# The scan of a two-block transformer kernel on one Trainium2 core: two carried parts added on VectorE before they reach TensorE

## The chip, the cores and the metric

The kernel runs on one core of one Trainium2 chip, in one launch. The metric is the device time of that launch in microseconds (us). Work is shared among five engines that have queues of their own and meet only at semaphores: TensorE (PE in the profile; its weight loads are PEld), VectorE (DVE), ScalarE (ACT), GpSimd (POOL) and SyncE (SP), which issues the DMAs. SBUF is the on-chip memory; PSUM, with eight banks of 512 f32 words per partition, takes the results of TensorE. Each queue is worked off in order, so an instruction that waits holds up all behind it on its engine.

## What is computed

Two transformer layers come first, with feed-forward parts, three kinds of attention and gates. A second block follows, on 256 tokens, and only one stage of it is touched: the bidirectional scan. For one direction, cut to what matters (chunks of 128 tokens, so two chunks; 12 heads of 64 channels in 4 groups that share B and C of 128 states):

```python
st = einsum('bcsgn,bcsgr,bcsgrp->bcgrpn', Bq, exp(a_end - a_cs), xq)      # what a chunk adds to the state
h_fin, h_in = scan(step, h0, (st, a_end))                                # state carried into each chunk
scores = einsum('bcqgn,bcsgn->bcqsg', Cq, Bq)                            # C and B
y_diag = einsum('bcqsg,bcqsgr,bcsgrp->bcqgrp', scores, decay, xq)        # within the chunk
y_off  = einsum('bcqgn,bcgrpn,bcqgr->bcqgrp', Cq, h_in, exp(a_cs))       # carried into the chunk
y = y_diag + y_off
```

This is done forward and backward and the two y are added. Then y + d_skip * x is gated by silu(z), normed over 768 channels and multiplied by the output weights, and the block goes on with a feed-forward part.

## The kernel before, in words

Activations lie with channels on the partitions and 256 tokens along the free dimension. Weights stream through a ring of five slabs of 128x2048 (`raw`); ScalarE writes the high part of each to `whi`, VectorE or GpSimd the rest to `wlo` (`cut_lo`; on GpSimd as two halves), and each f32 product is three matmuls (`block3`).

The scan has four steps e = 0 to 3: token chunk tt = e // 2, direction d = e % 2. For each step:

- `carried(e)` (TensorE, L1717): C times the carried state of the direction, 4 matmuls into PSUM banks 6 and 7.
- `carried_scale(e)` (VectorE, L2504): that product times exp(a_cs) per token and head, out of PSUM into `yoff` in SBUF, tokens on the partitions.
- `turned(e)` (TensorE, L1726): `yoff` times the identity, 6 matmuls, which turns it to channels on the partitions and adds it to y in banks 0 to 2. `turned(0)` opens the banks (start=True).
- `within_weights(e)` (VectorE, L2495): the decays `seg[e]` (128x1536) times the scores in PSUM, in place.
- `within(e)` (TensorE, L1735): 12 matmuls of 64 channels each that add the part within the chunk. Those of step 3 release `y_done`, three times.

The scores of both chunks (L1709, 8 matmuls, `cb_done`) come ahead of all this. The order on each engine is written out by hand. `carried(e)` waits until step e-1 has been read out of banks 6 and 7 (`yoff_ready`).

Between the steps VectorE has other work: `z_clamp(j)` for j = 1, 2 (L2455, 128x512), a clamp of z into `zex`, of which ScalarE makes a sigmoid (`z_sigmoid`, three activations) and GpSimd the product with z (`silu` of z, L633, `z_silu`). All three j share the one tile `zex`, so `z_clamp(1)` waits for `z_silu` 1, the product of j = 0, and `z_clamp(2)` for `z_silu` 2. GpSimd's queue here is: the fourfold product `xdt` (L544), the z product 0, the z product 1, the two halves of slab WOUT20+2, the z product 2, the two halves of slab WOUT20+3. VectorE also has `cut_lo` of slab WOUT20+1 (128x2048) and `ycat_low(0, ...)`, the low part of `u_t` (128x512, `hlo`).

Behind step 3 VectorE adds the skip part (L2531), multiplies by the gate, ScalarE squares, TensorE sums (L1574) while it works on the parts of the output product that are there (`wout`, L1165 to L1167), and the norm follows.

Of the kernel before, what the change touches and what calls it, by code (L numbers as in the profile page):

```python
# [18 lines left out]
ALU = mybir.AluOpType  # L19
# [3 lines left out]
P = 128  # L23
D = 1024
KT = D // P
S = 256
ST = S // P
# [24 lines left out]
WOUT20 = WIN20 + WIN2_SLABS  # L52
# [80 lines left out]
class Steps:  # L133
# [32 lines left out]
NG = 4  # L166
# [9 lines left out]
def build_program(nc, t):  # L176
# [31 lines left out]
    ident = sb("ident", [P, P])  # L208
# [86 lines left out]
    yoff = at("yoff", [P, 2, 768], F32, xw0)  # L295
# [20 lines left out]
    b_t = at("b_t", [P, NG, S], F32, a0 + 12288)  # L316
# [9 lines left out]
    xdt = at("xdt", [P, ST, 2, 768], F32, v0)  # L326
# [816 lines left out]
    def _(pe):  # L1143
# [559 lines left out]

        pe.wait_ge(conv_silu, NCONV)
        pe.wait_ge(h1_ready, 1)
        for tt in range(ST):
            for g in range(NG):
                tok = slice(tt * P, (tt + 1) * P)
                ins = pe.matmul(ps[:, 4 + tt, g * P:(g + 1) * P], b_t[:, g, tok], c_t[:, g, tok], start=True, stop=True)  # L1709
        ins.then_inc(cb_done, 1)  # L1710

        def carried(e):

            tt, d = e // 2, e % 2
            at_least(pe, yoff_ready, e)
            for g in range(NG):
                ins = pe.matmul(ps[:, 6 + g // 2, 192 * (g % 2):192 * (g % 2) + 192], c_t[:, g, tt * P:(tt + 1) * P],  # L1717
                                hstate[:, d, (tt if d == 0 else 1 - tt), 192 * g:192 * g + 192], start=True, stop=True)
            ins.then_inc(yoff_done, 1)

        def turned(e):

            tt = e // 2
            pe.wait_ge(yoff_ready, e + 1)
            for m in range(XC):
                pe.matmul(ps_flat[:, m * S + tt * P:m * S + (tt + 1) * P], yoff[:, e % 2, m * P:(m + 1) * P], ident[:, :],  # L1726
                          start=(e == 0 and m % 2 == 0), stop=False, skip_group_check=True)

        def within(e):

            tt, d = e // 2, e % 2
            pe.wait_ge(seg_ready, e + 1)
            for h in range(NH):
                out = ps[64 * (h % 2):64 * (h % 2) + 64, h // 4, (h // 2 % 2) * S + tt * P:(h // 2 % 2) * S + (tt + 1) * P]
                ins = pe.matmul(out, xdt[:, tt, d, 64 * h:64 * h + 64], seg[e][:, h, :], start=False, stop=(d == 1),  # L1735
                                skip_group_check=True)
                if e == 3 and h % 4 == 3:
                    ins.then_inc(y_done, 1)

        carried(0)  # L1740
        pe.wait_ge(uz_evac, 8)
        turned(0)
        carried(1)
        pe.wait_ge(xdt_ready, 1)
        within(0)
        turned(1)
        carried(2)
        within(1)
        turned(2)
        carried(3)  # L1750
        within(2)
        turned(3)
        within(3)

        def wout(q, first, last):
# [71 lines left out]
    def _(dve):  # L1827
# [3 lines left out]
        def tt_(out, a, b, op):  # L1831
            return dve.tensor_tensor(out, a, b, op)  # L1832
# [7 lines left out]
        def cut_lo(g):  # L1840

            if N_SLABS <= g < CTX0:
                return
            slot = PLACE[g] % NS
            dve.wait_ge(hi_done[slot], SPLITS[g])
            c = slice(PART if g in DT_SLABS else 0, SLAB)
            tt_(wlo[:, slot, c], raw[:, slot, c], whi[:, slot, c].bitcast(F32), ALU.subtract).then_inc(lo_done[slot], 1)
# [647 lines left out]
        def within_weights(e):  # L2495

            tt = e // 2
            s4 = seg[e][:, :, :].rearrange("p (g r) n -> p g r n", r=3)
            dve.wait_ge(cb_done, 1)
            dve.wait_ge(seg_exp, 3 * tt + 3)  # L2500
            tt_(s4, s4, ps[:, 4 + tt, :].rearrange("p (g n) -> p g n", n=P).unsqueeze(2).to_broadcast([P, NG, 3, P]),
                ALU.mult).then_inc(seg_ready, 1)

        def carried_scale(e):  # L2504

            dve.wait_ge(yoff_done, e + 1)
            form = "p b (h n) -> p b h n"
            tt_(yoff[:, e % 2, :].rearrange("p (b h n) -> p b h n", b=2, n=64), ps[:, 6:8, 0:384].rearrange(form, n=64),
                tail_x[:, 48 + 12 * e:60 + 12 * e].rearrange("p (b h) -> p b h", b=2).unsqueeze(3).to_broadcast([P, 2, 6, 64]),
                ALU.mult).then_inc(yoff_ready, 1)  # L2510

        def ycat_low(j, first, src):
            dve.wait_ge(ycat_hi_ready, j + 1)
# [3 lines left out]
        for e in range(4):  # L2517
            if e == 3:
                ycat_low(0, 0, u_t[:, :, :])
            carried_scale(e)  # L2520
            within_weights(e)
            if e == 0:
                z_clamp(1)
                cut_lo(b2 + WOUT20 + 1)
            if e == 1:
                z_clamp(2)

        for j in range(XC // 2):
            dve.wait_ge(y_done, j + 1)
# [240 lines left out]
```

## Time and profile before

| | us |
|---|---|
| runs of the kernel before | median 1632.33 (1631.1 to 1632.45) |
| the profiled execution | 1631.88 |
| its span in the trace | 1630.1 |
| TensorE matmuls busy | 1610.9 (99%) |
| VectorE busy | 1295.7 (79%) |
| ScalarE busy | 923.4 (57%) |
| GpSimd busy | 205.5 (13%) |
| stage of the scan (scores to the last within product) | 1380.15 to 1401.11 |

The times of rows are microseconds from the start of the span. A row of the timeline has the start, the length, the engine, the line, the operation, the tiles and the count; in brackets stands how long the engine was idle before it, and who ended that. Each f32 matmul shows as two passes, so x12 is six matmuls. An instruction of VectorE or GpSimd can begin some hundredths before the last one ends, and its length holds the time in which it is already issued but can't move.

### The profile page before, as it was taken

What the parts mean: (1) busy time and instruction counts of PE and PEld (TensorE: products, weight loads), DVE (VectorE), ACT (ScalarE), POOL (GpSimd) and SP (SyncE); (2) the same over time, 40 slices, a digit from 0 to 9 for tenths busy, and PEclk for the clock granted to TensorE, in tenths of its full rate; (3) what the DMA queues carried; (4) which work ended last, traced back from release to release, by engine and by line L of the source; (5) the groups of instructions that cost most, each with busy time, mean ns of one, the idle gap of its engine ahead of it and who ended that gap; (6) DMA issues with size and microseconds to landing.
All of it is one profiled execution on the core that took longest, in us unless ns stands there. A gap on an engine that the chain in (4) does not pass through costs nothing.

```text
span 1630.1 us, 29907 instructions
## 1 busy us (share of the span) xinstructions
PE 1610.9 (99%) x13152; PEld 1546.7 (95%) x13152; DVE 1295.7 (79%) x1458; ACT 923.4 (57%) x1094; POOL 205.5 (13%) x122
## 2 busy tenths in 40 slices
PE   8999999999999999999999999999999999999998
PEld 8999978999999999999988899999999988999998
DVE  8887878678889888897878678875898598796655
ACT  7554655675465455545656685464555557554544
POOL 1000100000140001200100000032323358400000
PEclk9999999999999999999999999999999999999999
DMA  7667654344556765776654434555554424135552
GB/s 293 230 259 288 236 185 175 140 146 159 219 220 235 279 237 198 283 259 253 264 187 175 150 134 158 193 217 191 197 198 165 152 107 155 70 138 185 204 185 75
DMA packets 47521, 317.58 MB, mean 195 GB/s; under 512 B 5280, under 2 KB 8096, under 8 KB 9888
## 3 DMA queue, kind: packets, MB, share of 16 engines
q1 hardware_dynamic: 47248, 315.64, 52.8%
q8 instruction: 104, 1.70, 0.4%
q14 instruction: 25, 0.20, 0.0%
q10 hardware_dynamic: 144, 0.02, 0.0%
HBM read 314.60 MB, written 1.05 MB: 194 GB/s over the span
## 4 chain that ended last, share of the span: by engine, by line
PE 90%; DVE 7%; ACT 2%; issue 1%; DMA 1%; SPq 0%; DVEq 0%; ACTq 0%
PE ps L1165 25%; PE ps L1166 25%; PE ps L1167 25%; PE ps L1363 3%; PE ps L1365 3%; PE ps L1364 3%; DVE wlo L1832 2%; PE ps L1377 1%; DVE pre L2443 1%; PE ps L1388 1%; DVE dA_rows L1832 1%; DVE tmp L1832 1%; DMA raw<-in_w_dram 1%; DVE qkA L1832 1%; PE ps L1584 0%
## 5 line engine op out<-in xcount | busy, mean ns | idle before, releaser
L1832 DVE TENSOR_TENSOR wlo<-raw,whi 128x2048 fp32r<-128x2048 f32 (+1 forms) x256 | 584.8, 2292 | 90.4 <-ACT whi L649 87.3
L649 ACT ACTIVATE whi<-raw 128x2048 fp32r<-128x2048 f32 (+1 forms) x264 | 500.1, 1906 | 215.0 <-DMA raw<-in_w_dram 214.6
L1165 PE MATMUL ps<-h1hi,whi 128*128 128x256 f32 x1792 | 500.2, 279 | 3.4 <-DVE wlo L1832 3.4
L1167 PE MATMUL ps<-h1lo,whi 128*128 128x256 f32 x1792 | 496.2, 277 | 0.0
L1166 PE MATMUL ps<-h1hi,wlo 128*128 128x256 f32 x1792 | 496.2, 277 | 0.0
L1165 PEld LDWEIGHTS ps<-h1hi,whi 128*128 128x128 f32 x1792 | 336.8, 188 | 7.0 <-DVE h1lo L1891 2.5
L1166 PEld LDWEIGHTS ps<-h1hi,wlo 128*128 128x128 f32 x1792 | 336.8, 188 | 0.1
L1167 PEld LDWEIGHTS ps<-h1lo,whi 128*128 128x128 f32 x1792 | 336.9, 188 | 0.0
L1165 PE MATMUL ps<-hid_hi,whi 128*128 128x256 f32 x880 | 243.7, 277 | 0.0
L1166 PE MATMUL ps<-hid_hi,wlo 128*128 128x256 f32 x880 | 243.0, 276 | 0.0
L1167 PE MATMUL ps<-hid_lo,whi 128*128 128x256 f32 x880 | 243.0, 276 | 0.0
L1165 PE MATMUL ps<-hhi,whi 128*128 128x256 f32 x672 | 188.1, 280 | 2.3 <-DVE hlo L2418 1.3
L1166 PE MATMUL ps<-hhi,wlo 128*128 128x256 f32 x672 | 186.2, 277 | 0.0
L1167 PE MATMUL ps<-hlo,whi 128*128 128x256 f32 x672 | 186.2, 277 | 0.0
L1165 PEld LDWEIGHTS ps<-hid_hi,whi 128*128 128x128 f32 x880 | 165.2, 188 | 0.3
L1166 PEld LDWEIGHTS ps<-hid_hi,wlo 128*128 128x128 f32 x880 | 165.3, 188 | 0.0
L1167 PEld LDWEIGHTS ps<-hid_lo,whi 128*128 128x128 f32 x880 | 165.2, 188 | 0.0
L550 POOL TENSOR_TENSOR sq<-sq 128x512 f32<-128x512 f32 x18 | 27.5, 1528 | 934.4 <-ACT sq L678 922.6
L1165 PEld LDWEIGHTS ps<-hhi,whi 128*128 128x128 f32 x672 | 126.6, 188 | 4.1 <-issue 2.3
L1166 PEld LDWEIGHTS ps<-hhi,wlo 128*128 128x128 f32 x672 | 126.3, 188 | 0.3
L1167 PEld LDWEIGHTS ps<-hlo,whi 128*128 128x128 f32 x672 | 126.2, 188 | 0.0
L683 ACT ACTIVATE t_exp<-t_exp 128x512 f32<-128x512 f32 x55 | 34.7, 632 | 145.2 <-DVE t_exp L1986 145.1
(365 smaller groups left out, 2624.8 us busy)
## 6 DMA issues: line engine op xcount, KB each, us to landing
raw<-in_w_dram SPq DMA_DIRECT2D x288, 1024.0 KB, 4.8
raw<-in_w_dram SPq DMA_DIRECT2D x8, 256.0 KB, 5.2
c_rows<-in_c_rows_dram SPq DMA_DIRECT2D x2, 1024.0 KB, 9.9
relbias<-in_relbias_dram SPq DMA_DIRECT2D x2, 1024.0 KB, 8.5
pv<-in_pv_dram SPq DMA_DIRECT2D x2, 641.0 KB, 6.9
xT<-in_x_dram SPq DMA_DIRECT2D x4, 256.0 KB, 4.6
raw<-in_w_dram SPq DMA_DIRECT2D x2, 512.0 KB, 6.0
ctxT<-in_ctx_dram SPq DMA_DIRECT2D x1, 1024.0 KB, 6.8
```

Of the source, the lines that this page charges most:

```text
L550: step.done(pool.tensor_tensor(sq[:, 0:2, :], sq[:, 0:2, :], sq[:, 2 * j:2 * j + 2, :], ALU.add))
L649: act.activation(whi[:, slot, c], raw[:, slot, c], ACT.Copy).then_inc(hi_done[slot], 1)
L683: step.done(act.activation(v, v, ACT.Exp, scale=-1.0))
L1165: pe.matmul(out, w_hi, hi, start=start, stop=False, skip_group_check=skip)
L1166: pe.matmul(out, w_lo, hi, start=False, stop=False, skip_group_check=skip)
L1167: return pe.matmul(out, w_hi, lo, start=False, stop=stop, skip_group_check=skip)
L1363: pe.matmul(out, h_hi, w_hi, start=(k == 0), stop=False)
L1364: pe.matmul(out, h_hi, w_lo, start=False, stop=False)
L1365: ins = pe.matmul(out, h_lo, w_hi, start=False, stop=(k == KT - 1))
L1377: ins = pe.transpose(ps_flat[:, first + j * P:first + (j + 1) * P], tile, ident[:, :])
L1388: ins = pe.matmul(ps_flat[:, c:c + width], qkT[rows, j, tt * P:(tt + 1) * P], qkT[rows, 4 + j, 0:width], start=True, stop=True)
L1832: return dve.tensor_tensor(out, a, b, op)
```

## The change

Three things are done.

1. The two directions of one chunk are added on VectorE. `carried_scale` for an even step writes the scaled product to `yoff[tt]` as before. For an odd step it scales the product in place in PSUM, waits for itself (`done`), and adds it to `yoff[tt]` in a further instruction. `turned` is then called twice, once for each chunk, in place of four times.
2. On TensorE `carried(0)` is put ahead of the scores, `carried(1)` behind them, `within(0)` opens the banks of y (start=True on the first matmul of each bank and partition half), and `turned(tt)` comes behind `within(0)` and `within(2)`.
3. On VectorE `z_clamp(1)` is put ahead of `within_weights(0)` and the cut of slab WOUT20+1 behind `within_weights(2)`, in place of behind `z_clamp(1)`.

```diff
-        for tt in range(ST):
-            for g in range(NG):
-                ...
-        ins.then_inc(cb_done, 1)
...
-        def turned(e):
-            tt = e // 2
-            pe.wait_ge(yoff_ready, e + 1)
+        def turned(tt):
+            pe.wait_ge(yoff_ready, 2 * tt + 2)
             for m in range(XC):
-                pe.matmul(ps_flat[...], yoff[:, e % 2, m * P:(m + 1) * P], ident[:, :],
-                          start=(e == 0 and m % 2 == 0), stop=False, skip_group_check=True)
+                pe.matmul(ps_flat[...], yoff[:, tt, m * P:(m + 1) * P], ident[:, :],
+                          start=False, stop=False, skip_group_check=True)
...
-                ins = pe.matmul(out, xdt[...], seg[e][:, h, :], start=False, stop=(d == 1), ...)
+                ins = pe.matmul(out, xdt[...], seg[e][:, h, :], start=(e == 0 and h % 4 < 2), stop=(d == 1), ...)
...
         carried(0)
+        for tt in range(ST):
+            for g in range(NG):
+                tok = slice(tt * P, (tt + 1) * P)
+                ins = pe.matmul(ps[:, 4 + tt, ...], b_t[:, g, tok], c_t[:, g, tok], start=True, stop=True)
+        ins.then_inc(cb_done, 1)
+        carried(1)
         pe.wait_ge(uz_evac, 8)
-        turned(0)
-        carried(1)
         pe.wait_ge(xdt_ready, 1)
         within(0)
-        turned(1)
         carried(2)
+        turned(0)
         within(1)
-        turned(2)
         carried(3)
         within(2)
-        turned(3)
+        turned(1)
         within(3)
...
             dve.wait_ge(yoff_done, e + 1)
-            tt_(yoff[:, e % 2, :]..., ps[:, 6:8, 0:384]..., tail_x[...]..., ALU.mult).then_inc(yoff_ready, 1)
+            product = ps[:, 6:8, 0:384]
+            both = yoff[:, e // 2, :].rearrange("p (b m) -> p b m", b=2)
+            ins = tt_((product if e % 2 else both)..., product..., tail_x[...]..., ALU.mult)
+            if e % 2:
+                done(ins)
+                ins = tt_(both, both, product, ALU.add)
+            ins.then_inc(yoff_ready, 1)
...
             carried_scale(e)
-            within_weights(e)
             if e == 0:
                 z_clamp(1)
-                cut_lo(b2 + WOUT20 + 1)
+            within_weights(e)
             if e == 1:
                 z_clamp(2)
+            if e == 2:
+                cut_lo(b2 + WOUT20 + 1)
```

On TensorE, from the first scores on, stood this before (`c_t` and `b_t` are C and B, `hstate` the carried states, `seg0` to `seg3` the weights of steps 0 to 3):

```order
L1709 MATMUL ps<-c_t_151,b_t_139 128x128 x8
L1717 MATMUL ps<-hstate_140,c_t_151 128x192 x4
L1726 MATMUL ps<-ident_56,yoff_123 128x128 x6
L1717 MATMUL ps<-hstate_140,c_t_151 128x192 x4
L1735 MATMUL ps<-seg0_162,xdt_146 64x128 x12
L1726 MATMUL ps<-ident_56,yoff_123 128x128 x6
L1717 MATMUL ps<-hstate_140,c_t_151 128x192 x4
L1735 MATMUL ps<-seg1_163,xdt_146 64x128 x12
L1726 MATMUL ps<-ident_56,yoff_123 128x128 x6
L1717 MATMUL ps<-hstate_140,c_t_151 128x192 x4
L1735 MATMUL ps<-seg2_164,xdt_146 64x128 x12
L1726 MATMUL ps<-ident_56,yoff_123 128x128 x6
```

(one more group, of `seg3`, ends the stage), and this stands there now, the whole stage:

```order
L1712 MATMUL ps<-hstate_140,c_t_151 128x192 x4
L1738 MATMUL ps<-c_t_151,b_t_139 128x128 x8
L1712 MATMUL ps<-hstate_140,c_t_151 128x192 x4
L1729 MATMUL ps<-seg0_162,xdt_146 64x128 x12
L1712 MATMUL ps<-hstate_140,c_t_151 128x192 x4
L1720 MATMUL ps<-ident_56,yoff_123 128x128 x6
L1729 MATMUL ps<-seg1_163,xdt_146 64x128 x12
L1712 MATMUL ps<-hstate_140,c_t_151 128x192 x4
L1729 MATMUL ps<-seg2_164,xdt_146 64x128 x12
L1720 MATMUL ps<-ident_56,yoff_123 128x128 x6
L1729 MATMUL ps<-seg3_165,xdt_146 64x128 x12
```

Two of four groups of turning matmuls are gone, and a carried product stands on both sides of the scores.

On VectorE, behind the scaling of step 0, stood this before:

```order
L1832 TENSOR_TENSOR seg0_162<-seg0_162,ps 128x1536
L2455 TENSOR_SCALAR zex_136<-z_t_130 128x512
L1832 TENSOR_TENSOR wlo_50<-raw_49,whi_51 128x2048
L1832 TENSOR_TENSOR yoff_123<-ps,small2_160 128x768
L1832 TENSOR_TENSOR seg1_163<-seg1_163,ps 128x1536
L2455 TENSOR_SCALAR zex_136<-z_t_130 128x512
L1832 TENSOR_TENSOR yoff_123<-ps,small2_160 128x768
L1832 TENSOR_TENSOR seg2_164<-seg2_164,ps 128x1536
L1832 TENSOR_TENSOR hlo_55<-u_t_166,hhi_54 128x512
L1832 TENSOR_TENSOR yoff_123<-ps,small2_160 128x768
L1832 TENSOR_TENSOR seg3_165<-seg3_165,ps 128x1536
```

and now, up to the last addition (`seg3` is right behind it):

```order
L2452 TENSOR_SCALAR zex_136<-z_t_130 128x512
L1829 TENSOR_TENSOR seg0_162<-seg0_162,ps 128x1536
L1829 TENSOR_TENSOR ps<-ps,small2_160 128x2x384
L1829 TENSOR_TENSOR yoff_123<-yoff_123,ps 128x768
L1829 TENSOR_TENSOR seg1_163<-seg1_163,ps 128x1536
L2452 TENSOR_SCALAR zex_136<-z_t_130 128x512
L1829 TENSOR_TENSOR yoff_123<-ps,small2_160 128x768
L1829 TENSOR_TENSOR seg2_164<-seg2_164,ps 128x1536
L1829 TENSOR_TENSOR wlo_50<-raw_49,whi_51 128x2048
L1829 TENSOR_TENSOR hlo_55<-u_t_166,hhi_54 128x512
L1829 TENSOR_TENSOR ps<-ps,small2_160 128x2x384
L1829 TENSOR_TENSOR yoff_123<-yoff_123,ps 128x768
```

The clamp stands ahead of `seg0`, the cut of the slab has moved from ahead of step 1 to directly ahead of `hlo` and step 3, and each odd step has one instruction more. The queues of ScalarE, GpSimd and SyncE are as before.

## Rows read from the trace of the kernel before

**Rows 1.** The page, the chain that ended last, shares by engine.

```profile
PE 90%; DVE 7%; ACT 2%; issue 1%; DMA 1%; SPq 0%; DVEq 0%; ACTq 0%
```

**Rows 2.** Timeline of TensorE, the scan: start us, length us, engine, what.

```profile
1380.15 1.95 PE L1709 MATMUL ps<-c_t,b_t 128*128 128x128 f32 x16
1381.93 1.47 PE L1717 MATMUL ps<-hstate,c_t 128*128 128x192 f32 x8
1384.54 1.57 PE L1726 MATMUL ps<-ident,yoff 128*128 128x128 f32 x12 [1.14 <-DVE yoff L1832]
...
1387.35 1.53 PE L1735 MATMUL ps<-seg,xdt 128*64 128x128 f32 x24
1389.52 1.60 PE L1726 MATMUL ps<-ident,yoff 128*128 128x128 f32 x12 [0.64 <-DVE yoff L1832]
...
1399.65 1.53 PE L1735 MATMUL ps<-seg,xdt 128*64 128x128 f32 x24
1401.11 0.38 PE L1165 MATMUL ps<-hhi,whi 128*128 128x256 f32 x1
```

**Rows 3.** The chain of waits, a piece behind the scan: start us, us, what.

```profile
1404.20 2.63 PE ps L1574 x12
```

**Rows 4.** Timeline of VectorE, the scan and what follows it.

```profile
1383.44 0.96 DVE L1832 TENSOR_TENSOR yoff<-ps,small 128x768 f32<-128x768 f32 x1 [3.00 <-PE ps L1717]
1384.31 1.74 DVE L1832 TENSOR_TENSOR seg<-seg,ps 128x1536 f32<-128x1536 f32 x1
1385.97 0.42 DVE L2455 TENSOR_SCALAR zex<-z_t 128x512 f32<-128x512 f32 x1
1386.31 2.29 DVE L1832 TENSOR_TENSOR wlo<-raw,whi 128x2048 fp32r<-128x2048 f32 x1
...
1391.04 1.29 DVE L2455 TENSOR_SCALAR zex<-z_t 128x512 f32<-128x512 f32 x1
1392.46 0.96 DVE L1832 TENSOR_TENSOR yoff<-ps,small 128x768 f32<-128x768 f32 x1
...
1395.00 1.35 DVE L1832 TENSOR_TENSOR hlo<-u_t,hhi 128x512 fp32r<-128x512 f32 x1
...
1400.35 0.87 DVE L2531 SCALAR_TENSOR_TENSOR xs_t<-xs_t,pc,ps 128x256 f32<-128x256 f32 x2 [0.98 <-PE ps L1735]
...
1407.82 0.42 DVE L1836 SCALAR_TENSOR_TENSOR rsqb<-rsqa 128x256 f32<-128x256 f32 x1
1408.27 0.43 DVE L1832 TENSOR_TENSOR rsqb<-rsqb,var 128x256 f32<-128x256 f32 x1
```

**Rows 5.** Timeline of GpSimd, the scan.

```profile
1384.59 1.27 POOL L633 TENSOR_TENSOR z_t<-z_t,zex 128x512 f32<-128x512 f32 x1
...
1389.69 2.36 POOL L538 TENSOR_TENSOR wlo<-raw,whi 128x1024 fp32r<-128x1024 f32 x1
1392.00 2.56 POOL L538 TENSOR_TENSOR wlo<-raw,whi 128x1024 fp32r<-128x1024 f32 x1
1394.53 1.26 POOL L633 TENSOR_TENSOR z_t<-z_t,zex 128x512 f32<-128x512 f32 x1
1395.76 2.81 POOL L538 TENSOR_TENSOR wlo<-raw,whi 128x1024 fp32r<-128x1024 f32 x1
```

**Rows 6.** Timeline of VectorE, a feed-forward part some 190 us earlier.

```profile
1197.37 3.77 DVE L1832 TENSOR_TENSOR wlo<-raw,whi 128x2048 fp32r<-128x2048 f32 x1
1201.07 2.88 DVE L1832 TENSOR_TENSOR hid_lo<-t_hid,hid_hi 128x512 fp32r<-128x512 f32 x1
```

**Rows 7.** Timeline of GpSimd, the same stretch.

```profile
1196.14 2.85 POOL L538 TENSOR_TENSOR wlo<-raw,whi 128x1024 fp32r<-128x1024 f32 x1
1198.96 4.45 POOL L538 TENSOR_TENSOR wlo<-raw,whi 128x1024 fp32r<-128x1024 f32 x1
```

**Rows 8.** Busy by stretch (PE, PEld, DVE, ACT, POOL), then granted clock, DMA share, GB/s.

```profile
1380.00:1402.00 22.00, 20.22 (x202) 18.41 (x201) 17.45 (x17) 6.61 (x10) 18.28 (x10) 1.00 0.20 81
```

**Rows 9.** The waits of TensorE in the whole span: total, times, longest us.

```profile
PE ps L1270 <- issue: 1.8, 1, 1.8
```

More of the change, by code:

```diff
@@ L1705, in _ @@
         pe.wait_ge(h1_ready, 1)
-        for tt in range(ST):
-            for g in range(NG):
-                tok = slice(tt * P, (tt + 1) * P)
-                ins = pe.matmul(ps[:, 4 + tt, g * P:(g + 1) * P], b_t[:, g, tok], c_t[:, g, tok], start=True, stop=True)
-        ins.then_inc(cb_done, 1)
         def carried(e):
@@ L1719, in carried @@
             ins.then_inc(yoff_done, 1)
-        def turned(e):
-            tt = e // 2
-            pe.wait_ge(yoff_ready, e + 1)
+        def turned(tt):
+            pe.wait_ge(yoff_ready, 2 * tt + 2)
             for m in range(XC):
-                pe.matmul(ps_flat[:, m * S + tt * P:m * S + (tt + 1) * P], yoff[:, e % 2, m * P:(m + 1) * P], ident[:, :],
-                          start=(e == 0 and m % 2 == 0), stop=False, skip_group_check=True)
+                pe.matmul(ps_flat[:, m * S + tt * P:m * S + (tt + 1) * P], yoff[:, tt, m * P:(m + 1) * P], ident[:, :],
+                          start=False, stop=False, skip_group_check=True)
         def within(e):
@@ L1734, in within @@
                 out = ps[64 * (h % 2):64 * (h % 2) + 64, h // 4, (h // 2 % 2) * S + tt * P:(h // 2 % 2) * S + (tt + 1) * P]
-                ins = pe.matmul(out, xdt[:, tt, d, 64 * h:64 * h + 64], seg[e][:, h, :], start=False, stop=(d == 1),
-                                skip_group_check=True)
+                ins = pe.matmul(out, xdt[:, tt, d, 64 * h:64 * h + 64], seg[e][:, h, :], start=(e == 0 and h % 4 < 2),
+                                stop=(d == 1), skip_group_check=True)
                 if e == 3 and h % 4 == 3:
@@ L1740, in _ @@
         carried(0)
+        for tt in range(ST):
+            for g in range(NG):
+                tok = slice(tt * P, (tt + 1) * P)
+                ins = pe.matmul(ps[:, 4 + tt, g * P:(g + 1) * P], b_t[:, g, tok], c_t[:, g, tok], start=True, stop=True)
+        ins.then_inc(cb_done, 1)
+        carried(1)
         pe.wait_ge(uz_evac, 8)
-        turned(0)
-        carried(1)
         pe.wait_ge(xdt_ready, 1)
         within(0)
-        turned(1)
         carried(2)
+        turned(0)
         within(1)
-        turned(2)
         carried(3)
         within(2)
-        turned(3)
+        turned(1)
         within(3)
@@ L2507, in carried_scale @@
             form = "p b (h n) -> p b h n"
-            tt_(yoff[:, e % 2, :].rearrange("p (b h n) -> p b h n", b=2, n=64), ps[:, 6:8, 0:384].rearrange(form, n=64),
-                tail_x[:, 48 + 12 * e:60 + 12 * e].rearrange("p (b h) -> p b h", b=2).unsqueeze(3).to_broadcast([P, 2, 6, 64]),
-                ALU.mult).then_inc(yoff_ready, 1)
+            product = ps[:, 6:8, 0:384]
+            both = yoff[:, e // 2, :].rearrange("p (b m) -> p b m", b=2)
+            ins = tt_((product if e % 2 else both).rearrange(form, n=64), product.rearrange(form, n=64),
+                      tail_x[:, 48 + 12 * e:60 + 12 * e].rearrange("p (b h) -> p b h", b=2).unsqueeze(3)
+                      .to_broadcast([P, 2, 6, 64]), ALU.mult)
+            if e % 2:
+                done(ins)
+                ins = tt_(both, both, product, ALU.add)
+            ins.then_inc(yoff_ready, 1)
         def ycat_low(j, first, src):
```

## The prediction

> **What bounds the kernel now.** I read the page first. The chain that ended last is TensorE's for 90% of the span [rows 1], so a microsecond taken from TensorE counts only where TensorE is what the stage waits for, and one that it must wait anew counts in full. Then I laid the timelines of the stage side by side. TensorE goes from the scores at 1380.15 to the first output product at 1401.11, 20.96 us, and is idle twice, 1.14 and 0.64 us, each time for VectorE's `yoff` [rows 2]. So before, TensorE bounds the scan and VectorE is just behind: its clamp of z at 1391.04 is followed only at 1392.46 by the next scaling, as soon as the carried product is there. Behind the scan the chain goes on through the skip part at 1400.35 [rows 4] and the sums of squares [rows 3], so a delay of step 3 reaches the end of the kernel undiminished.
>
> **TensorE alone would gain.** Twelve turning matmuls go, two groups of 12 passes at about 1.41 us from start to start (I read 1.57 and 1.60 with the drain [rows 2]): 2.8 us. The two idle times, 1.8 us, could go too. That is the ceiling, 4.6 us. All of it is hidden if VectorE is late, so I walk VectorE's new queue.
>
> **VectorE, step by step.** An instruction starts some 0.08 us before the last ends, so I use start-to-start lengths: scaling 0.87, `seg` 1.66, clamp 0.34 (the first three rows and the fourth [rows 4]).
>
> 1. `carried(0)` now starts at 1380.15 and takes 1.47, so its scaling runs from 1381.66 instead of 1383.44 [rows 2, 4]. A head start of 1.8 us.
> 2. `z_clamp(1)` is next, and it waits for z product 0, since both use `zex`. GpSimd runs that from 1384.59 to 1385.86 [rows 5], and nothing in the change makes it earlier: it follows the `xdt` product in GpSimd's own queue. Before, the clamp stood at 1385.97, behind `seg0`, where the wait was already over [rows 4]. Now VectorE stands idle from 1382.6 to 1385.93, and `seg0` is queued behind the wait: it starts at 1386.27, not 1384.31, and `within(0)` at 1388.07, not 1387.35 [rows 2, 4]. The head start is gone and 0.7 us more. The scores end near 1383.5, so they hold up nothing.
> 3. Step 1: the scaling in PSUM from 1387.93, 0.96 long, then the addition. A dependent pair follows with a gap of 0.03 (1407.82 + 0.42 to 1408.27 [rows 4]). The addition also reads 768 elements, one operand from PSUM; I take 0.96 again. It ends at 1389.87. Neither instruction is in the trace. The bounds for each are 0.9 and 1.74, the latter a `seg` row, with twice the elements; I take 0.96, the row of the same size and the same source. Then `seg1` from 1389.8 to 1391.53.
> 4. `z_clamp(2)` is issued at 1391.45. Before, it was issued at 1391.04 and ended at 1392.33, 0.28 behind the end of GpSimd's half slab (1389.69 + 2.36 = 1392.05), though by itself it takes 0.42 [rows 4, 5]. The half slab of GpSimd holds it, and it does so again: end 1392.3. The scaling of step 2 starts at 1392.22 (its product, behind the addition of step 1, is ready at 1391.5), 0.24 earlier than before. `seg2` runs from 1393.1 to 1394.84.
> 5. The slab cut is issued at 1394.76. Before, it ran at 1386.31, where GpSimd was idle, in 2.29 us [rows 4]. Now GpSimd is in z product 2, until 1395.79 [rows 5], and its half slabs are queued behind that. What comes of this I read from an earlier place with the same three instructions [rows 6, 7]: a cut issued at 1197.37 waited for the GpSimd half that ended at 1198.99 and ended 2.15 later at 1201.14; the second half, issued at 1198.96, waited for it and took 4.45; and the 128x512 low part that VectorE issued at 1201.07 waited for that half and took 2.88, not 0.69 or so. So the two take turns, whole instructions long. Here: the cut ends at 1395.76 + 2.15 = 1397.9; `hlo`, issued at 1397.83, takes 2.88 and ends at 1400.71 (before: 1.35 at 1395.00 [rows 4]).
> 6. Step 3: scaling from 1400.63 to 1401.59, addition to 1402.58, `seg3` from 1402.5 to 1404.24, `within(3)` at 1404.3 against 1399.65 [rows 2].
>
> One rule speaks against this change. The trace has the turns: 3.77, 4.45 and 2.88 us [rows 6, 7]. The Trainium skill, "SBUF — State Buffer", section "SBUF: two separate sides", says that a VectorE instruction with two SBUF inputs or in a two-port mode and a GpSimd instruction share a pair of ports that one of them holds to its end. The trace agrees, and the forecast would be the same by it; what it adds is that the two new additions, with one input in PSUM, should pay nothing to GpSimd (if they did, each could wait up to a half slab, 2.4 us).
>
> **The sum.** Counted on VectorE's queue against the rows of before [rows 2, 4]:
> - up to the end of step 2: the head start of 1.8, the wait behind it, the cut out of this stretch and one addition into it leave VectorE 0.24 us earlier (1394.76 against 1395.00), since both times GpSimd's half slab releases the clamp;
> - the cut, now here: 1397.83 - 1394.76 = 3.07;
> - from `hlo`'s start to `within(3)`: before 1399.65 - 1395.00 = 4.65; now 2.80 for `hlo`, 0.99 for the scaling with its gap, 0.88 for the addition, 1.80 for `seg3` and its signal, 6.47 in all: 1.82 more.
>
> -0.24 + 3.07 + 1.82 = 4.65 us. TensorE's path fits below: it is done with `within(2)` at 1397.1 and waits for the addition at 1402.58; `turned(1)` ends at 1404.0, still ahead of `seg3`. So nothing of TensorE's gain arrives. Against the profiled 1631.88 this gives 1636.5; the median of the runs is 0.45 higher, 1632.33, so I forecast 1636.9.
>
> What hides what: the cut itself is needed only by the second output product, some 2 us behind `within(3)`; GpSimd's last half, shifted to 1403.1, ends before VectorE's next instruction with two SBUF operands (the gate product, then near 1405.9).
>
> **Rivals.**
> - *A. As above.* 1636.9. Own range 1636 to 1638.
> - *B. The clock.* TensorE would now be idle twice for long, 1384.8 to 1388.1 and 1397.1 to 1402.6. The longest idle time of its matmuls in the trace is 1.8 us [rows 9], and the granted clock is 1.00, the 2.4 GHz level, throughout the scan [rows 8]; no row shows what 5.5 us do. If the clock falls to 1.2 GHz, `turned(1)` takes 2.8, ends at 1405.45 and passes `seg3` by 1.2 us, and the first third of `within(3)` takes 0.5 more: +1.7, 1638.6. If it stays low through the 24 output products behind (2.93 us, 1401.11 to about 1404.04 [rows 2, 3]), these cover the chain no more and it is up to +5.4, 1642.3. The Trainium skill, "TensorE: Matmul & The Clock Gate", section "What's actually happening", has the clock halved after idling and given back after sustained work; no run here shows it so far.
> - *C. The clamp slips a turn.* If scaling in PSUM costs over 0.6 us more than 0.96, `z_clamp(2)` is issued behind 1392.05, GpSimd's second half goes first, and everything from there moves by about 2.3 us: 1639.2. Against it: it takes most of the bound of 1.74.
> - *D. VectorE keeps its turn.* If `hlo` goes ahead of the waiting half, it costs 0.6 and not 2.88: 1634.6. Against it: the row of 2.88. With no waits for GpSimd at all from step 4 on, VectorE alone would bring `within(3)` to 1400.8, +1.15: 1633.5.
> - *E. Faster.* TensorE's list decides, and its 4.6 us arrive: 1627.7. The place is `z_clamp(1)`: it would have to find `zex` free at 1382.6, and the cut its turn at once. Even then VectorE's own instructions, from `seg0` at 1383.6 on, end only 2.7 earlier than in the last case of D, 1630.8. Only if the two PSUM instructions cost well under 0.9 each does it go further.
>
> **Chances.** A 0.50, B 0.20, C 0.07, D 0.16 (both forms), E and anything that is faster 0.04, others slower 0.03. About 0.2%, 3.3 us, is what a measurement of this kernel tells from no change. A, B, C and the others are slower by more than that, 0.80, of which a hundredth goes to A's low end; D is within it, with a hundredth of A and one of E, 0.18; faster by over 0.2% keeps 0.03. The range goes from the better form of D to B's first size with a margin: 1634.0 to 1640.0, which leaves out the second form of D, E, and B where the clock stays low.
>
> **What would show it.** In the new profile: VectorE idle about 3.3 us ahead of the clamp of z, released by GpSimd's z product, and `seg0` after 1386; the slab cut near 1394.8 with 3.1 us in place of 2.29; `hlo` near 2.9 us; TensorE idle about 3.3 us before `within(0)` and 5.5 before `turned(1)`, both for VectorE. The lengths of the two new VectorE instructions decide C; the granted clock behind 1402 decides B. I am wrong if TensorE's idle time before the last turning is under 2 us, or if `hlo` is short.

## The result and the profile after

The changed kernel takes 1638.04 us in the median of 5 runs (1637.4 to 1640.7), against 1632.33 us before (5 runs, 1631.1 to 1633.11): ratio 1.0040, interval 1.0028 to 1.0051 (ratios here are taken over all runs; the two medians alone give 1.0035). It is slower by 5.7 us. The forecast was 1636.9 with a range of 1634.0 to 1640.0. The profiled execution is the slowest of the five, 1640.7 us with a span of 1638.9, so its trace shows more than the median has to lose; a run further down shows the rest.

The stage starts at 1379.51 here and at 1380.15 before [rows 2], 0.64 us apart for reasons ahead of the change, so I compare distances from the first matmul of the stage. Step 3's products start 27.59 us behind it, against 19.50 before: 8.1 us later. TensorE's timeline, output products left out (three dots stand for rows left out, here as below):

```profile
1379.51 1.47 PE L1712 MATMUL ps<-hstate,c_t 128*128 128x192 f32 x8
1380.81 1.95 PE L1738 MATMUL ps<-c_t,b_t 128*128 128x128 f32 x16
1382.60 1.47 PE L1712 MATMUL ps<-hstate,c_t 128*128 128x192 f32 x8
1387.54 2.83 PE L1729 MATMUL ps<-seg,xdt 128*64 128x128 f32 x24 [3.47 <-DVE seg L1829]
1390.29 2.87 PE L1712 MATMUL ps<-hstate,c_t 128*128 128x192 f32 x8
...
1404.24 2.93 PE L1720 MATMUL ps<-ident,yoff 128*128 128x128 f32 x12 [5.32 <-DVE yoff L1829]
1407.10 2.83 PE L1729 MATMUL ps<-seg,xdt 128*64 128x128 f32 x24
```

Two things are to be seen, which answer to the two idle times of 1.14 and 0.64 us in [rows 2]. TensorE now waits 3.47 us for the weights of step 0 and 5.32 us for the last addition. And behind each wait it is slow: 24 passes of `within(0)` take 2.83 us, not 1.53, and 8 passes of `carried(2)` 2.87, not 1.47. The granted clock by stretch says the same (the third last column; before it was 1.00 throughout [rows 8]):

```profile
1380.00:1385.00 5.00, 4.06 (x31) 3.77 (x29) 0.96 (x1) 2.01 (x2) 5.00 (x4) 1.00 0.77 301
1385.00:1388.00 3.00, 0.47 (x5) 0.49 (x7) 2.70 (x3) 1.89 (x3) 0.40 (x2) 0.69 0.00 0
1388.00:1393.00 5.00, 5.00 (x32) 4.67 (x30) 3.62 (x4) 1.26 (x2) 5.00 (x3) 0.50 0.00 0
1393.00:1398.00 5.00, 5.00 (x57) 4.48 (x58) 4.80 (x3) 1.15 (x2) 5.00 (x4) 1.00 0.00 0
...
1404.00:1406.00 2.00, 1.76 (x8) 1.76 (x9) 1.85 (x2) 0.00 (x0) 0.00 (x0) 0.50 0.00 0
```

The clock falls to 1.2 GHz (0.50) in both idle times. It is still there when step 3's products run: 24 passes take 2.83 us in place of 1.53. So behind step 3 more is lost. ScalarE's `rsqa`, the first step of the norm behind the sums, starts 36.05 us behind the stage's start here and 26.71 before: 9.3 us later, not 8.1. VectorE's timeline, which answers to [rows 4]:

```profile
1381.01 0.96 DVE L1829 TENSOR_TENSOR yoff<-ps,small 128x768 f32<-128x768 f32 x1 [1.23 <-PE ps L1712]
1385.30 0.43 DVE L2452 TENSOR_SCALAR zex<-z_t 128x512 f32<-128x512 f32 x1 [3.33 <-POOL z_t L633]
1385.64 1.75 DVE L1829 TENSOR_TENSOR seg<-seg,ps 128x1536 f32<-128x1536 f32 x1
1387.31 0.96 DVE L1829 TENSOR_TENSOR ps<-ps,small 128x768 f32<-128x768 f32 x1
1388.30 0.95 DVE L1829 TENSOR_TENSOR yoff<-yoff,ps 128x768 f32<-128x768 f32 x1
...
1393.20 0.96 DVE L1829 TENSOR_TENSOR yoff<-ps,small 128x768 f32<-128x768 f32 x1 [1.54 <-PE ps L1712]
...
1395.74 3.84 DVE L1829 TENSOR_TENSOR wlo<-raw,whi 128x2048 fp32r<-128x2048 f32 x1
1399.50 2.82 DVE L1829 TENSOR_TENSOR hlo<-u_t,hhi 128x512 fp32r<-128x512 f32 x1
...
1404.10 1.75 DVE L1829 TENSOR_TENSOR seg<-seg,ps 128x1536 f32<-128x1536 f32 x1
```

The 3.33 us ahead of the clamp, released by GpSimd's z product, are there; so are the two new instructions with 0.96 and 0.95 us, the long cut (3.84, where 2.29 stood) and the long low part (2.82, where 1.35 stood). One wait is new to me: 1.54 us ahead of the scaling of step 2, for the carried product that ran at the lower clock. And GpSimd's two half slabs, which answer to the last row of [rows 5]:

```profile
1395.06 2.36 POOL L538 TENSOR_TENSOR wlo<-raw,whi 128x1024 fp32r<-128x1024 f32 x1
1397.38 4.39 POOL L538 TENSOR_TENSOR wlo<-raw,whi 128x1024 fp32r<-128x1024 f32 x1
```

Since the cut came 1.6 us later in the stage than I had it (16.23 against 14.61 from its start), the first half had already begun; the cut waited for its end, 1397.42, and the second half stood against the low part. The chain of waits has it all in one column:

```profile
1382.54 1.43 POOL xdt L544
1383.97 1.23 POOL z_t L633
1385.36 0.28 issue
1385.64 1.76 DVE seg L1829
...
1387.54 2.83 PE ps L1729 x24
1390.36 2.81 PE ps L1712 x8
...
1395.82 3.75 DVE wlo L1829
1399.57 2.75 DVE hlo L1829
```

Before, the same view had VectorE in the chain only at step 0:

```profile
1384.31 1.60 DVE seg L1832
...
1386.39 1.10 DVE wlo L1832
...
1389.52 1.60 PE ps L1726 x12
```

With the clamp between them (0.42 us) and the scaling at 1388.51 (0.96) that makes 4.1 us; from 1389.52 to the first output product the chain was TensorE's. Now the chain goes through GpSimd, VectorE, TensorE at the lower clock, and VectorE again.

### The profile page after: what moved, and what is told of

The parts are those of the page before. It is cut to its first block, busy times and chain, and to the rows that moved or that the text cites. A ratio compares the mean times of both kernels' runs of the same rounds, so it can differ in the third digit from the quotient of the medians.

```text
span 1638.9 us, 29860 instructions
## 1 busy us (share of the span) xinstructions
PE 1614.7 (99%) x13128; PEld 1551.2 (95%) x13128; DVE 1299.6 (79%) x1460; ACT 923.3 (56%) x1094; POOL 207.8 (13%) x122
## 4 chain that ended last, share of the span: by engine, by line
PE 84%; DVE 10%; ACT 2%; issue 1%; DMA 1%; POOL 1%; SPq 0%; DVEq 0%; ACTq 0%; POOLq 0%
PE ps L1165 23%; PE ps L1166 23%; PE ps L1167 23%; PE ps L1363 3%; PE ps L1365 3%; PE ps L1364 3%; DVE pre L2440 2%; DVE wlo L1829 2%; PE ps L1377 1%; DMA raw<-in_w_dram 1%; PE ps L1388 1%; DVE cex L2446 1%; ACT whi L649 1%; DVE dA_rows L1829 1%; DVE tmp L1829 1%
```

## The experiments

Three groups of four kernels, each group on one chip beside runs of the kernel before (medians 1631.72, 1631.17 and 1631.83 us). My theory: VectorE's queue sets step 3, by the clamp's wait, by the cut and the low part taking turns with GpSimd, and by the additions, and the lower clock comes on top. The rivals: the clock is most of it; the additions are; TensorE's new order is. In each profile I measured from the first matmul of the stage to the first product of step 3. The third column is the median less that of the kernel before in the same group:

| kernel | median us | above its before | ratio, interval | stage to step 3, us | against before |
| --- | --- | --- | --- | --- | --- |
| before | 1632.33 |  |  | 19.50 |  |
| changed | 1638.04 | +5.71 | 1.0040, 1.0028 to 1.0051 | 27.59 | +8.09 |
| changed, once more | 1639.58 | +7.75 | 1.0054, 1.0042 to 1.0067 | 27.56 | +8.06 |
| both fillers | 1636.50 | +4.78 | 1.0026, 1.0014 to 1.0038 | 23.93 | +4.43 |
| both fillers, once more | 1636.23 | +4.40 | 1.0033, 1.0020 to 1.0045 | 23.90 | +4.40 |
| first filler alone | 1637.62 | +5.79 | 1.0038, 1.0025 to 1.0051 | 25.50 | +6.00 |
| clamp back | 1639.26 | +7.54 | 1.0043, 1.0028 to 1.0057 | 25.07 | +5.57 |
| cut back | 1635.76 | +4.04 | 1.0021, 1.0012 to 1.0029 | 23.94 | +4.44 |
| both back | 1634.57 | +2.85 | 1.0020, 1.0010 to 1.0031 | 21.70 | +2.20 |
| slab given to VectorE, fillers | 1633.08 | +1.91 | 1.0012, 1.0003 to 1.0022 | 22.17 | +2.67 |
| own tile for the clamp | 1636.02 | +4.85 | 1.0029, 1.0017 to 1.0040 | 22.94 | +3.44 |
| TensorE's order alone | 1631.62 | +0.45 | 1.0003, 0.9994 to 1.0012 | 19.58 | +0.08 |
| the mix | 1629.23 | -1.94 | 0.9987, 0.9978 to 0.9995 | 16.66 | -2.84 |
| the mix, four turnings | 1630.22 | -1.61 | 0.9989, 0.9980 to 0.9998 | 18.25 | -1.25 |

The distance is that of one execution each; the median is that of all runs, of which only the profiled one has a trace. A part of each distance has nothing to do with the edits: in the kernels that leave GpSimd's queue and `zex` alone, z product 0 starts 4.18 to 4.62 us behind the stage's start (4.44 before, 4.43 in the changed kernel, 4.23 with both fillers). So differences of 0.2 us say little. Medians of different groups are from different chips, so they are compared by the third column.

### Fillers: the clock taken out

```diff
         carried(1)
         pe.wait_ge(uz_evac, 8)
+        filler(12)       # 12 times: pe.matmul(ps[:, 3, 0:P], ones[:, :], ident[:, :], start=True, stop=True)
         pe.wait_ge(xdt_ready, 1)
         within(0)
         ...
         within(2)
+        filler(22)
         turned(1)
```

> The changed kernel with TensorE kept busy where it waits: 12 matmuls of ones times identity (24 passes of about 0.11 us) ahead of the first within product and 22 ahead of the second turning, into a PSUM bank that nobody reads. If VectorE's queue sets step 3 and the clock came on top (my theory), the clock stays at its upper level, step 3 starts about 4.65 us later than in the kernel before, and the time is 1636 to 1637 with less scatter than the changed kernel's 1637.4 to 1640.7. If the lower clock is most of the loss, it falls to 1633 or 1634. If the clock costs nothing in the median, it is 1638.

Measured: 1636.50 us. The distance to step 3 is 4.43 us longer than before, where my sum had 4.65. This is the run that shows the sum bare. I had expected less scatter too, and there was none of that: its 12 runs lie between 1634.55 and 1642.82. VectorE in it:

```profile
1395.48 3.16 DVE L1836 TENSOR_TENSOR wlo<-raw,whi 128x2048 fp32r<-128x2048 f32 x1
1398.57 2.83 DVE L1836 TENSOR_TENSOR hlo<-u_t,hhi 128x512 fp32r<-128x512 f32 x1
1401.33 0.95 DVE L1836 TENSOR_TENSOR ps<-ps,small 128x768 f32<-128x768 f32 x1
1402.31 0.95 DVE L1836 TENSOR_TENSOR yoff<-yoff,ps 128x768 f32<-128x768 f32 x1
```

and TensorE, without the output products:

```profile
1385.44 2.84 PE L1737 MATMUL ps<-ident,ones 128*128 128x128 f32 x24
1388.89 1.53 PE L1729 MATMUL ps<-seg,xdt 128*64 128x128 f32 x24 [0.61 <-DVE seg L1836]
...
1397.92 5.18 PE L1737 MATMUL ps<-ident,ones 128*128 128x128 f32 x44
1403.32 1.60 PE L1720 MATMUL ps<-ident,yoff 128*128 128x128 f32 x12 [0.22 <-DVE yoff L1836]
1404.99 1.53 PE L1729 MATMUL ps<-seg,xdt 128*64 128x128 f32 x24
```

The cut, issued 14.42 us behind the stage's start (I had 14.61), takes 3.16 (3.15 by my walk), the low part 2.83 (2.88). Every TensorE group has its full-speed length again, and the granted clock is 1.00 in every stretch from 1378 to 1414. "The clock is most of it" is out: with the clock at its upper level, 4.4 us remain, in the stage and up to `rsqa` (31.14 us against 26.71).

What the clock costs needed one chip for all, so the last group has the changed kernel unaltered, both fillers again, and the first filler alone (`filler(12)` and no `filler(22)`).

> The changed kernel, unaltered, on the same chip as the runs with fillers, so that the clock has a price: in its first profiled execution the granted clock was at the lower level twice and step 3 started 27.6 us after the stage's start, against 23.9 us with fillers. Theory: about 1.5 us slower than the run with both fillers in the median, with single runs between 0.5 and 4 us slower; the profile shows lower clock behind one or both idle times of TensorE. Rival (the clock is back before it matters in most runs): the two medians within 0.5 us.

> The changed kernel with the 12 fillers ahead of the first within product alone; the idle time of 5.5 us ahead of the last turning stays. Theory: no lower clock near the first carried products, step 3 still behind a turning at the lower clock: 0 to 1.5 us below the changed kernel and about 1 to 1.5 above the run with both fillers. Rival (only the first idle time costs): as with both fillers.

> The run with both fillers once more, beside the changed kernel: 4.4 to 4.9 us above the kernel before, ratio about 1.0028, with the clock at its upper level throughout the scan.

Measured: 1639.58, 1637.62 and 1636.23 us. Between the first and the last lie 3.35 us, more than the 1.5 I expected, and more than half of that (1.96, where I had at most 1.5) is gone with the first filler. The kernel with both fillers is 4.40 us above the kernel before, as expected. The intervals of neighbours overlap (1.0042 to 1.0067, 1.0025 to 1.0051, 1.0020 to 1.0045), so how the cost divides between the two idle times isn't settled by the runs, nor is the rival that only the first one costs. In the earlier groups the changed kernel was 5.71 and the one with fillers 4.78 above its own runs of before, 0.9 us apart. So the size stays rough: 0.9 to 3.4 us in the median.

The traces are sharper. The two profiles of the changed kernel agree in 0.03 us (27.59 and 27.56). Against the fillers the first has step 3 3.66 us later. The end of the low part is 2.47 us later already (22.81 against 20.34 us behind the stage's start): 0.2 of that is the earlier z product 0, the rest is the first idle time's share, which came through `carried(2)`, the scaling and the cut. The other 1.19 are the last turning at the lower clock. Another 1.25 us goes behind step 3, 4.9 in all up to `rsqa`. The first filler alone takes most of the first share away (the low part ends 20.72 us behind the stage's start) and leaves the last turning as it was, step 3 at 25.50 us:

```profile
1401.31 2.93 PE L1720 MATMUL ps<-ident,yoff 128*128 128x128 f32 x12 [5.31 <-DVE yoff L1836]
```

### The clamp back behind the weights

```diff
             carried_scale(e)
+            within_weights(e)
             if e == 0:
                 z_clamp(1)
-            within_weights(e)
```

> The changed kernel with the clamp of z for pair 1 back behind the weights of step 0. Theory: the first weights start near 1383.6 and TensorE's first long idle time (3.3 us) is gone, but the second clamp is still released by the end of the same half slab of GpSimd, so step 2, the cut, the low part and step 3 stand where they stood: 4.65 us later than before plus what the second idle time costs in clock, 1637 to 1638.5. Rival (delays of VectorE add up): the 1.96 us of the first weights come back in full, about 1635 to 1636.

Measured: 1639.26 us, no faster than the changed kernel, beyond the range I gave by 0.8. Its VectorE:

```profile
1383.61 1.75 DVE L1829 TENSOR_TENSOR seg<-seg,ps 128x1536 f32<-128x1536 f32 x1 [0.83 <-PE ps L1738]
...
1389.78 2.48 DVE L2452 TENSOR_SCALAR zex<-z_t 128x512 f32<-128x512 f32 x1
1392.19 0.94 DVE L1829 TENSOR_TENSOR yoff<-ps,small 128x768 f32<-128x768 f32 x1
```

The weights of step 0 start 3.28 us behind the stage's start, not 6.13 as in the changed kernel, and all that is won waits inside the second clamp, 2.48 us long for an instruction that takes 0.43 alone: it is issued 0.15 us behind the start of GpSimd's half slab (1389.63) and stays until that ends. So the delays do not add up, and the rival (1635 to 1636) is wrong. (GpSimd's z product 1, too, runs where it did: 8.07 us behind the stage's start, 8.09 with the fillers.) TensorE, done earlier, is idle for 6.17 us before the last turning, which then runs at the lower clock (12 passes in 2.93 us).

The cut is issued 14.38 us behind the stage's start, as with both fillers (14.42), so VectorE's queue is the same from there on. The kernel with fillers is 2.8 us faster in the median on the same chip. The difference that the traces show is the lower clock behind that last idle time; in the profile it is 1.7 us up to `rsqa`, and why the median of the clamp-back runs lies higher still is open.

### The cut back in step 0, and both back

```diff
             within_weights(e)
+            if e == 0:
+                cut_lo(b2 + WOUT20 + 1)
             ...
-            if e == 2:
-                cut_lo(b2 + WOUT20 + 1)
```

That is the first kernel. The second has `within_weights(e)` back ahead of `z_clamp(1)` as well, so VectorE's queue is that of before but for the additions.

> The changed kernel with the cut of the slab back in step 0 (behind the weights of step 0), the clamp left ahead of them. Theory: the cut runs at once from 1387.9, the low part waits only for the third z product, step 3 starts about 2.2 us later than before: 1634.5, up to 1635.5 if the clock falls in the first idle time. Rival (the place of the cut is indifferent, it is the two additions that cost): as the changed kernel, 1637 to 1638.

> The changed kernel with both moves of VectorE's queue undone: the two additions, the two turnings fewer and TensorE's new order stay. Theory: step 3 starts 0.2 to 0.4 us later than before, 1632.6; 1634.9 if the second clamp, issued at 1392.0 by my walk, comes behind the end of GpSimd's half slab (1392.05) and loses its turn. Rival (the additions cost 2 us on the chain): 1634.3 without such a lost turn. Rival (TensorE's 2.8 us arrive): 1629.5.

Measured: 1635.76 and 1634.57 us. Both are faster than the changed kernel, and both are slower than before, by more than the first forecast of each. In both the second clamp lost its turn, which I had reckoned with for the second kernel only. The first kernel, then the second:

```profile
1386.80 2.29 DVE L1829 TENSOR_TENSOR wlo<-raw,whi 128x2048 fp32r<-128x2048 f32 x1
...
1392.53 2.60 DVE L2452 TENSOR_SCALAR zex<-z_t 128x512 f32<-128x512 f32 x1
```

```profile
1391.17 2.60 DVE L2452 TENSOR_SCALAR zex<-z_t 128x512 f32<-128x512 f32 x1
```

2.60 us is 2.3 for the second half slab, which went ahead, and the clamp itself. With that the both-back kernel lands at +2.20 us in the stage, near its second forecast (0.3 + 2.3).

The first kernel needs care. Its step 3 stands at 23.94 us, where the changed kernel with fillers has it too (23.93), and the medians of the two on one chip are 0.7 us apart. So the cut back in its place didn't by itself bring step 3 forward: the cut is 2.29 us again and the low part 1.34, so 2.4 us are won there, but 1.8 are lost in the clamp that missed its turn, and 0.5 ahead of the scaling of step 3:

```profile
1399.48 0.97 DVE L1829 TENSOR_TENSOR ps<-ps,small 128x768 f32<-128x768 f32 x1 [0.48 <-PE ps L1712]
```

It waits there for `carried(3)`, which is late because `carried(2)` and the first turning run at the lower clock (2.93 and 2.76 us). What it has over the changed kernel is that TensorE is no longer idle for 5 us ahead of the last turning, which runs at full speed (1.60 us).

The both-back kernel has VectorE's old order and one addition more ahead of the clamp, 0.99 us, and loses 2.2: an instruction is paid for here in whole turns of its neighbour. The rival of the additions costing 2 us on the chain isn't excluded by the time alone (1634.3 against 1634.57); the row of 2.60 is what tells them apart.

### The slab that stood against the low part

GpSimd's last slab (WOUT20+3) is cut by VectorE behind the gate products; fillers 12 and 12.

```diff
-        cut_lo(b2 + WOUT20 + 3)                      # GpSimd
         cut_lo(b2 + FFN30)
 ...
             tt_(y2, y2, xs_t[...], ALU.mult).then_inc(y_gated, 1)
+        cut_lo(b2 + WOUT20 + 3)                      # VectorE
```

> The changed kernel with the last slab of GpSimd (WOUT20+3) cut by VectorE behind the three gate products, where it is idle for about 2.5 us, so that no half slab stands against the low part of u_t; with fillers on TensorE (12 and 12 matmuls) against the clock. Theory: the moved cut still waits for the third z product and takes 3.1 us, the low part takes 0.6 to 0.7 in place of 2.8, step 3 starts 2.4 us later than before: 1634.8. Rival (the turn with GpSimd is not what makes the low part long): as the run with fillers alone.

Measured: 1633.08 us, ratio 1.0012 (1.0003 to 1.0022). In the stage +2.67 us, where I had 2.4. The 1634.8 I gave was reckoned from 1632.33; this group's kernel before stands at 1631.17, so the runs are 1.9 us above it, less than the 2.4. VectorE:

```profile
1393.25 3.17 DVE L1835 TENSOR_TENSOR wlo<-raw,whi 128x2048 fp32r<-128x2048 f32 x1
1396.34 0.68 DVE L1835 TENSOR_TENSOR hlo<-u_t,hhi 128x512 fp32r<-128x512 f32 x1
```

The low part takes 0.68 us, not 2.83, with nothing else changed ahead of it. So it was the waiting half slab that made it long. The cut still takes 3.17, for the z product.

### A tile of its own for the clamp

```diff
+    zex_b = at("zex_b", [P, 2, S], F32, a0 + 7168)
+    zexs = (zex, zex_b, zex)
...
-            at_least(dve, z_silu, j)
+            if j == 1:
+                dve.wait_ge(conv_silu, NCONV)
+            if j == 2:
+                dve.wait_ge(z_silu, 1)
```

and the sigmoid, the z product and the clamp of pair j use `zexs[j]`.

> The changed kernel with a tile of its own for the clamp of pair 1, so that it waits for no z product; nothing is moved. Theory: the clamp runs near 1383.2, the first weights start near 1383.6, all of the z work of GpSimd comes 1 us or more earlier, and step 3 starts 2.4 us later than before: 1634.8, up to 1636 with the lower clock in TensorE's idle time ahead of the last turning. Rival (the cut and the low part alone make the loss): unchanged against the changed kernel.

Measured: 1636.02 us, ratio 1.0029. The number is at the edge of the forecast only because this chip is faster: against its own runs of before it is +4.85, where I had 2.4 to 3.7. The clamp is issued 2.4 us behind the stage's start and no longer waits for a product. In the stage it is +3.44. Of this the last turning at the lower clock is 1.2, since `seg3` was ready at 1402.28 and step 3 started at 1403.53:

```profile
1400.67 2.93 PE L1722 MATMUL ps<-ident,yoff 128*128 128x128 f32 x12 [5.79 <-DVE yoff L1831]
```

That leaves 2.2, near the forecast's 2.4. The cut and the low part are as long as ever (3.16 and 2.82). So the shared tile is a real part, 2.2 of the 4.4 us, but only a part; by the traces "the cut and the low part alone make the loss" is wrong (by the runs alone it isn't excluded, as the ratio's interval, 1.0017 to 1.0040, overlaps that of the changed kernel).

Why does this gain arrive, when the clamp put back behind the weights gained nothing? It comes through GpSimd. With its own tile the clamp of pair 1 no longer follows z product 0, so GpSimd's z product 1 runs 5.92 us behind the stage's start and not 8.09 (fillers) or 8.07 (clamp back). Its half slabs come 2.2 us earlier with it, and so does the release of the second clamp.

### TensorE's order alone

The kernel before with the scores behind the first carried product, `within(0)` opening the banks, four turnings (each behind a within product) and VectorE's queue untouched.

> The kernel before with TensorE's new order alone: scores behind the first carried product, within products open y's banks; four turnings, no additions, VectorE's queue as before. Theory: the stage stays bound by TensorE's 19 us of work and the clamp's release, 0.1 to 0.3 us faster, 1632.1: no change that can be told. Rival (the order is what costs): slower by over 1 us.

Measured: 1631.62 us, ratio 1.0003 (0.9994 to 1.0012), stage +0.08. No cost and no gain of the order can be told.

### A mix that beats both

```diff
-            if e == 3:
-                ycat_low(0, 0, u_t[:, :, :])        # VectorE; now behind step 3's weights
             carried_scale(e)
             if e == 0:
                 z_clamp(1)                          # into its own tile
             within_weights(e)
             if e == 1:
                 z_clamp(2)
-            if e == 2:
-                cut_lo(b2 + WOUT20 + 1)             # now GpSimd, ahead of its z product 2
```

Slab WOUT20+2 stays with GpSimd, behind z product 2, and slab WOUT20+3 goes to VectorE behind the gate products. The second kernel is the same with four turnings and no additions.

> Additions and TensorE's new order kept, the clamp of pair 1 ahead with a tile of its own; slab WOUT20+1 cut by GpSimd ahead of slab WOUT20+2, slab WOUT20+3 by VectorE behind the gate products, the low part of u_t behind the weights of step 3. Theory: VectorE has no cut and no wait for zex in the scan, TensorE's shorter list decides, step 3 starts 3 us earlier than before: 1629.3. Rival (VectorE's turns with GpSimd at the gate products, or the last slab coming late, give it back): 1631 to 1633.

> The mix of the last batch (own tile for the clamp, slabs cut elsewhere, low part behind step 3) with four turnings and no additions on VectorE. Theory: with VectorE out of the way the two turnings cost TensorE their 2.8 us, half of which fits in idle time: step 3 starts about 18.2 us after the stage's start, against 16.7 us with the additions and 19.5 us in the kernel before; ratio about 0.9992. Rival (the additions save nothing even here): ratio 0.9987 as the mix with additions, step 3 after 16.7 us.

Measured: 1629.23 us, ratio 0.9987 (0.9978 to 0.9995), and 1630.22 us, 0.9989 (0.9980 to 0.9998). Both are faster than the kernel before, by 1.9 and 1.6 us of the medians in their groups. TensorE in the mix:

```profile
1384.75 1.53 PE L1731 MATMUL ps<-seg,xdt 128*64 128x128 f32 x24 [0.76 <-DVE seg L1831]
...
1394.43 1.60 PE L1722 MATMUL ps<-ident,yoff 128*128 128x128 f32 x12 [0.58 <-DVE yoff L1831]
1396.10 1.53 PE L1731 MATMUL ps<-seg,xdt 128*64 128x128 f32 x24
```

With both long waits gone (0.76 and 0.58 us are left) the distance is 16.66 us with additions (forecast: 3 us less than 19.50) and 18.25 without (forecast: 18.2): the additions are worth 1.6 us in the stage once VectorE has room. Not all of it arrives. From the stage's start to the first step of the norm behind the sums (ScalarE's `rsqa`) it is 24.97 and 25.46 us, 26.71 before: 1.74 and 1.25 won. Without additions all of the 1.25 arrives; with them 1.1 of 2.84 is lost, and their worth up to `rsqa` is 0.5 us, not 1.6. The reason is on VectorE behind step 3, where the low part has to wait for GpSimd and the skip part is queued behind it, 1.82 us behind the start of step 3's products and not 0.70 as before and in the mix with four turnings. In the mix with additions:

```profile
1395.96 2.04 DVE L1831 TENSOR_TENSOR hlo<-u_t,hhi 128x512 fp32r<-128x512 f32 x1
1397.92 0.86 DVE L2537 SCALAR_TENSOR_TENSOR xs_t<-xs_t,pc,ps 128x256 f32<-128x256 f32 x2
```

The two medians are from different chips and their intervals overlap, so the runs alone don't rank the mixes.

## Why the prediction was right, and where it was off

- *TensorE alone would gain, and VectorE hides it.* Right. TensorE's list is 2.8 us shorter, by my estimate, and it waits 3.47 and 5.32 us instead of 1.14 and 0.64. That "TensorE bounds the scan" before was too simple: the chain of waits goes through VectorE for 4.1 us at step 0.
- *Step 2 of the walk, the clamp's wait.* Right in size: 3.33 us idle, where I had about 3.3, released by the z product.
- *Step 3, the new instructions.* 0.96 and 0.95 against the 0.96 taken for each; the bound of 1.74 played no part, so rival C did not happen in the changed kernel. Its mechanism, the clamp that slips a turn, did in two of the experiments.
- *Steps 4 and 5, the turns.* Right where the clock stays up: 4.43 and 4.40 against 4.65 us. The 0.2 between them lies ahead of the cut and is no more than the shift of z product 0 (4.23 against 4.44 us). In the profile of the changed kernel the cut met the first half slab instead of the z product (3.84 us long against 3.15), because the lower clock had made it late.
- *Rival D* (VectorE keeps its turn) is out by the 2.82 us of the low part, and by its 0.68 when the half slab was taken away. (By its own numbers D comes to 1634.7 rather than 1634.6, as 4.65 on 1632.33 gives 1637.0 rather than 1636.9; nothing hangs on either.)
- *Rival B, the clock*, is what was mis-sized. I gave it a chance of 0.20 and one place, the last turning, +1.7 (and up to 5.4 if the clock stayed low). The turning itself was priced rightly: it passes `seg3` by 1.2 us, and the skip part comes 0.5 us later behind step 3. It was there in both profiles of the changed kernel, and at two places: behind the first idle time as well, where it delays `carried(2)` (2.87 us against 1.47), through it the scaling of step 2 (1.54 us idle) and so the cut. I had named that idle time, 3.3 us, and then priced only the longer one. It costs 0.9 to 3.4 us in the median; without it the forecast's sum stands within 0.3 us, with it the result lies 1.1 above the forecast and inside the range.
- *How much of it was luck.* The forecast itself has no clock in it. The result, 1638.04, lies just outside case A's own range (1636 to 1638), and the whole range holds it because its upper end was made for B. The same kernel once more was 7.75 us above its runs of before, which on the 1632.33 of the first would be 1640.1, at the very end of the range. So VectorE's queue was forecast, and the clock, which the sum leaves out, cost little enough in the first five runs for the result to stay inside.

The rule of the Trainium skill on the clock ("TensorE: Matmul & The Clock Gate", section "What's actually happening"), that it is halved after idling and given back after sustained work, agrees with these traces. In each profile looked at here, the idle times of TensorE in the scan from 3.26 to 6.17 us were followed by 0.50 in the granted clock, and those of 1.2 us or less never brought the clock down. The other ("SBUF — State Buffer", section "SBUF: two separate sides"), that VectorE with two inputs in SBUF and GpSimd share a pair of ports that one of them holds to its end, agrees too: the low part takes 2.82 us with a half slab waiting and 0.68 without, and the addition with one input in PSUM takes 0.95 while GpSimd works (1388.30).

What stays open: what the additions alone cost in the changed kernel, since no run takes them out of it and leaves the rest (each is 0.95 us long in its rows); and how the clock's cost is spread over single executions. The changed kernel's ten runs lie between 1637.4 and 1642.5, but only two were looked at in a trace, both the slowest of their five. The scatter doesn't help: the kernel before spreads over 2.0 to 8.8 us in the four groups, and the kernel with both fillers over 8.3.

## What to carry to other kernels

An instruction taken from TensorE is a gain only if the engine that feeds it has as much room; walk that engine's queue first, instruction by instruction, with every wait that a moved instruction now meets early. Between VectorE and GpSimd count turns, not lengths: a cut or low part (two inputs in SBUF) and the clamp of 128x512 (one) each waited for the neighbour's whole instruction. A clamp issued just as a half slab ended (1391.17 against 1391.18 in the both-back kernel) let the next one go first and took 2.60 us. Ask, too, what sets the moment of a wait's release: a gain ahead of it that doesn't move the release is lost. And where a change leaves TensorE idle for as long as here (3.3 us and more), put a price on the lower clock behind each such gap, the short one as well as the long one.

## What the runs showed of the hardware that was not expected

- VectorE scaling 128x768 f32 from PSUM into the same place in PSUM takes 0.95 to 0.97 us, as much as from PSUM into SBUF (0.96).
- A clamp of 128x512 that takes 0.43 us alone was seen at 0.82, 1.31, 2.48 and 2.60 us (changed kernel, own tile, clamp back, both back), by where in GpSimd's instruction it was issued.
- Each idle time of TensorE of 3.26 to 3.47 us (changed kernel, cut back, both back) was followed by several microseconds at 1.2 GHz; 24 passes of a filler in a gap of 3.4 us kept 2.4 GHz (both runs with fillers: granted clock 1.00).
